# Attention stage: the low part of the queries on GpSimd, gate evictions between maxima and scalings, and four gate tiles moved into two pairs behind the convolution

## The reference, cut to what matters

```
h = rms_norm(x);  u = h @ w_in            # columns: V, B, C, Z (conv), q, k, v, z_a, gate_logits
y_c = b_c * causal_depthwise_conv(c_c * v_c) * silu(z_c);   y_a = y_c @ w_conv_out
scores = q @ k.T * scale   (blocks of 128 queries against 256 keys, 16 query heads, 4 key heads)
m = max(max(scores), sink);  p = exp(scores - m) / (sum + exp(sink - m));   o = p @ v
y_b = (o * silu(z_a)) @ w_attn_out
gates = sigmoid(gate_logits + gate_b);  merged = g_a * y_a + g_b * y_b;   x + merged @ w_out
```

## Time and profile before

| what | value |
|---|---|
| median of 3 runs | 2354.08 us (2352.46 to 2355.7) |
| profiled execution: its time, its span | 2355.41 us, 2353.7 us |
| PE busy | 2329.4 us, 99% of the span |
| DVE busy | 1616.4 us, 69% |
| ACT busy | 1029.6 us, 44% |
| GpSimd busy | 160.4 us, 7% |

### The profile page before, as it was taken

How to read it: one execution, slowest core, us unless ns; L and a number is a source line. 1 busy time by engine, 2 the same in 40 slices (tenths; PEclk the granted TensorE clock), 3 DMA queues, 4 the chain that set the end, 5 groups by cost and what they waited for, 6 DMA issues and landing times.

```text
span 2353.7 us, 30640 instructions
## 1 busy us (share of the span) xinstructions
PE 2329.4 (99%) x11180; PEld 1936.9 (82%) x11180; DVE 1616.4 (69%) x2561; ACT 1029.6 (44%) x1795; POOL 160.4 (7%) x227
## 2 busy tenths in 40 slices
PE   8999999999999999999999999999999999999998
PEld 6778888888888888888788888998888888888786
DVE  6759998567777766736555753473598888886655
ACT  6347666343443434422243343363355444452334
POOL 1000000100000021121000030021100000001000
PEclk9999999999999999999999999999999999999999
DMA  5112232452332264421110042362122222245333
GB/s 199 45 45 73 81 117 73 143 125 81 105 93 81 90 230 128 151 64 50 45 45 28 24 148 75 96 233 72 50 67 90 80 80 80 80 143 179 102 104 125
DMA packets 255894, 230.64 MB, mean 98 GB/s; under 512 B 7726, under 2 KB 226051, under 8 KB 254754
## 3 DMA queue, kind: packets, MB, share of 16 engines
q1 hardware_dynamic: 233920, 148.39, 20.8%
q0 software_dynamic: 19104, 69.12, 9.1%
q10 hardware_dynamic: 2754, 11.58, 1.5%
HBM read 177.68 MB, written 51.38 MB: 97 GB/s over the span
## 4 chain that ended last, share of the span: by engine, by line
PE 92%; DVE 5%; ACT 1%; DMA 1%; issue 1%; SPq 0%; ACTq 0%; DVEq 0%
PE bank L1194 9%; PE bank L1195 9%; PE bank L1196 9%; PE bank L1851 5%; PE bank L1852 5%; PE bank L1853 5%; PE bank L1429 4%; PE bank L1427 4%; PE bank L1428 4%; PE bank L1379 3%; PE bank L1378 3%; PE bank L1377 3%; PE bank L1662 1%; PE bank L1664 1%; PE bank L1663 1%; PE bank L1353 1%
## 5 line engine op out<-in xcount | busy, mean ns | idle before, releaser
L2027 ACT ACTIVATE whi<-wraw 128x1024 fp32r<-128x1024 f32 (+2 forms) x139 | 139.4, 1003 | 305.8 <-PE bank L1196 184.9
L3168 DVE TENSOR_TENSOR wlo<-wraw,whi 128x1024 fp32r<-128x1024 f32 (+1 forms) x154 | 180.0, 1169 | 110.2 <-ACT whi L2027 104.2
L1377 PE MATMUL bank<-xhi,whi 128*128 128x512 f32 x320 | 124.7, 390 | 0.0
L1379 PE MATMUL bank<-xhi,wlo 128*128 128x512 f32 x320 | 124.6, 389 | 0.0
L1378 PE MATMUL bank<-xlo,whi 128*128 128x512 f32 x320 | 124.6, 389 | 0.0
L1194 PE MATMUL bank<-x2hi,whi 128*128 128x512 f32 x240 | 94.5, 394 | 0.0
L1195 PE MATMUL bank<-x2lo,whi 128*128 128x512 f32 x240 | 94.1, 392 | 0.0
L1196 PE MATMUL bank<-x2hi,wlo 128*128 128x512 f32 x240 | 94.0, 392 | 0.0
L3924 DVE TENSOR_TENSOR resid<-bank,resid 128x512 f32 x32 | 22.1, 691 | 99.1 <-PE bank L1196 97.1
L1851 PE MATMUL bank<-x4hi,a_hi 128*128 128x512 f32 x228 | 88.8, 389 | 0.5 <-ACT ffn_u L2941 0.5
L1851 PE MATMUL bank<-t_hi,s_hi 128*128 128x512 f32 x228 | 88.8, 389 | 0.5 <-DVE t_lo L4321 0.5
(11 more groups left out here) (649 smaller groups left out, 6921.9 us busy)
## 6 DMA issues: line engine op xcount, KB each, us to landing
wraw<-in_w_in_dram SPq DMA_DIRECT2D x85, 512.0 KB, 3.9
wraw<-in_ffn_w_up_dram SPq DMA_DIRECT2D x44, 512.0 KB, 3.8
ffn_spill<-ffn_value SPq DMA_DIRECT2D x22, 512.0 KB, 3.4
filler_spill<-filler POOLq DMA_DIRECT2D x20, 512.0 KB, 2.9
wraw<-in_xattn_wkv_dram SPq DMA_DIRECT2D x16, 512.0 KB, 4.0
wraw<-in_ffn_w_down_dram SPq DMA_DIRECT2D x16, 512.0 KB, 4.4
wraw<-in_ffn_w_down_dram SPq DMA_DIRECT2D x16, 384.0 KB, 3.5
xraw<-in_x_dram SPq DMA_DIRECT2D x4, 1024.0 KB, 10.8
```

The lines of the kernel that those rows point to most:

```text
L1377: pe.matmul(ps(fill_bank(m)), whi[slot][:, k, :], xh, start=(k == 0), stop=False)
L1379: last = pe.matmul(ps(fill_bank(m)), wlo[slot][:, k, :], xh, start=False, stop=(k == KT - 1))
L3168: dve.tensor_tensor(wlo[slot][:, 0:n, :], wraw[slot][:, 0:n, :], whi[slot][:, 0:n, :].bitcast(F32), ALU.subtract).then_inc(s_wlo, 1)
```

## The change

- The low part of the queries, `unit_lo(u)`, goes from DVE to GpSimd, with the same waits and counts; there it stands ahead of the stores of unit u-1, and `store_o` and the load of x follow.
- 16 fillers in place of 20: 12 inside the 32 units (6 steps in each) in place of 16, and four behind as before. The four tiles taken out (two of each gate) become two more pairs behind the convolution: 18 pairs in place of 16.
- DVE evicts a half that is due in unit u-1 between `maxima(u-1)`/`turned_lo(u-2)` and `normalise(u-1)`, also when it is an early one; an early split too is made there, one unit later than before. With 12 tiles, 24 halves fall in 24 of the 32 iterations, always behind the maxima and ahead of the scalings. Of the 11 splits in the units, seven stand behind `sum_o` (DVE iterations 3, 8, 11, 16, 19, 24, 27) and four ahead of the scalings (iterations 6, 14, 22, 30; ACT's part of these falls in units 5, 13, 21, 29).

```diff
-FILL_TILES = [Z_A + n for n in range(8)] + [G_B + n for n in range(6)] + [G_A + n for n in range(6)]
-EXTRA_PAIRS = ((G_B + 6, G_B + 7), (G_A + 6, G_A + 7))
+FILL_TILES = [Z_A + n for n in range(8)] + [G_B + n for n in range(4)] + [G_A + n for n in range(4)]
+EXTRA_PAIRS = tuple((g + n, g + n + 1) for n in (4, 6) for g in (G_B, G_A))
 FILLERS = len(FILL_TILES)
-FILL_IN = 16
+FILL_IN = 12
...
-            for u in range(UNITS):
+            def unit_lo(u):
+
+                b, g = u // KV, u % KV
+                q = 64 * (g % 2)
+                pool.wait_ge(s_phi, u + 1)
+                pool.tensor_tensor(qlo[g % 2][q:q + 64, :].rearrange("p (h n) -> p h n", h=4),
+                                   q32[q:q + 64, g // 2, :, b * P:(b + 1) * P],
+                                   qhd[g % 2][q:q + 64, :].bitcast(F32).rearrange("p (h n) -> p h n", h=4),
+                                   ALU.subtract).then_inc(s_plo, 1)
+
+            def fillers_of(u):
+
                 for m in range(1, 2 * FILL_IN, 2):
                     if HALVES_DONE[m][0] == u:
                         store_filler(m // 2)
+
+            for u in range(UNITS):
+                unit_lo(u)
+                fillers_of(u - 1)
                 if u % KV == 2 and u > KV:
                     store_o(u // KV - 1)
                 if u == 5 * KV:
                     load_x_again(0)
+            fillers_of(UNITS - 1)
             load_x_again(1)
...
                 if u >= 2:
                     turned_lo(u - 2)
-                unit_lo(u)
                 if u >= 1:
+                    halves_due(u - 1, True)
+                    splits_due(u - 1, True)
                     halves_due(u - 1, False)
                     normalise(u - 1, (u - 1) % 2)
...
                 splits_due(u, False)
-                halves_due(u, True)
-                splits_due(u, True)
```

More of the change, by code:

```diff
@@ L590, in hybrid_then_mixer_kernel @@
         RING = 16 * FILLERS // 4
-        BACK = (RING + 16, RING + 16, RING, RING, 16 * 3, 16 * KT, 16 * KT, 32 * KT)
+        BACK = (RING + 16, RING + 16, RING + 16, RING + 16, 16 * 3, 16 * KT, 16 * KT, 32 * KT)
         GATES, VO0 = s_vo_stored, 16 * KT
@@ L3335, in _ @@
                 value_lo(c)
[L3337 to L3344, removed]
             def sum_o(u):
@@ L3436, in _ @@
             maxima(UNITS - 1)
+            turned_lo(UNITS - 2)
+            halves_due(UNITS - 1, True)
+            splits_due(UNITS - 1, True)
             halves_due(UNITS - 1, False)
-            turned_lo(UNITS - 2)
             normalise(UNITS - 1, (UNITS - 1) % 2)
```

## The result

The changed kernel takes 2389.2 us (median of 4 runs, 2387.88 to 2391.5) against 2354.08 before: a ratio of 1.015, 95% interval 1.0133 to 1.0168, so slower by 1.5%. The forecast was 2376.3 with a range of 2358 to 2390: the result lies 0.8 us inside its upper end and above the 2368 to 2384 that the forecast gave its own case. Its sum was made for the profiled execution, and there it said +22.2 us; measured were 2387.88 - 2355.41 = +32.5. The sign and the place were right, a third of the size was missing. One execution of the later kernel e5_splits_behind took 3340 us at a granted clock of 0.65, where the others of all kernels had 0.99 to 1.00, and its ratio leaves it out.

A forecast was written before the change was run, and what follows sets the result against it. The DVE and ACT loop was taken to bound the units: -29.5 us for the attention stage, +38.1 for the pairs and +13.6 for holds made +22.2, so 2376.3 us, range 2358 to 2390.

The forecast's parts named there:

- PE's work, -5.4 us, and the pairs, +38.1: Whole kernel: four tiles less and two convolution pairs more cut PE's work by 5.4 us; the pairs alone add 38.1.
- The loop bounds the units: Units: maxima, exponentials, normalise, sum_o and load_rq on DVE and ACT take 6.85 us plus splits; iterations 3 to 31: 209.6.
- Evictions in the hole cost nothing: DVE waits for ACT's exponentials from 2.25 to 4.47 us after the maxima's start; evictions of 0.61 us there are free.
- The holds, 13.6 us: Units: DVE's small SBUF operations wait for GpSimd's whole unit_lo, 13.6 us in all, bounds 0 and 28.5.
- Behind a split: Seven iterations with a split behind sum_o: the split keeps GpSimd off, so load_rq is not held; 0, up to 10 us.
- Odd copies: Seven plain odd iterations: load_rq starts 0.09 us after GpSimd; half counted as held at 1.2 us, 4.2 in all.
- Even copies: Four plain even iterations: load_rq starts inside unit_lo and is held, +0.95 us each, 3.8 in all.
- Behind `store_o`: Seven iterations: unit_lo, late after the store's issue, meets the maxima's small operations; 0.8 us each, 5.6 in all.
- Head -2.0: First units: PE would save 4.1 us; half, 2.0, was estimated, with bounds 0 and 4.1.
- The second: Units: all odd copies held and GpSimd slipping in behind each split; +36, 2390 us; chance 0.12.
- Rival 1: Units: the DVE and ACT loop bounds them but GpSimd holds nobody; +8.6 up to +14, 2363 to 2368 us; chance 0.27.
- Rival 3: Units: PE paces them at 6.83 us and keeps its 5.4 us saving; 2348.7 us; chance 0.14.

The follow-up runs named there:

- e5_splits_behind: Changed kernel with load_rq behind the scalings, store_o one unit later and all 11 splits behind sum_o: 2371.74 us, ratio 1.0067 against the kernel before.
- e2: Changed kernel with unit_lo back on DVE behind turned_lo, all else as changed: 2373.36 us, ratio 1.0079 against the kernel before.
- e6: e5_splits_behind without load_rq, the maxima reading their factor from rq itself: 2367.6 us, ratio 1.0051 against the kernel before.
- e1: Changed kernel with load_rq moved from ahead of the maxima to behind the scalings, ahead of sum_o: 2373.11 us, ratio 1.0086 against the kernel before.
- e3: Kernel before with only unit_lo moved to GpSimd, 16 tiles still in the units: 2358.34 us, ratio 1.0017 against the kernel before.
- e4: Changed kernel with load_rq behind the scalings, store_o one unit later, seven splits moved from behind sum_o to ahead of the next scalings: 2373.94 us, ratio 1.0083.
- e7: e6 with 13 filler tiles in the units, three behind, and the last filler's eviction ahead of the convolution's sums: 2358.82 us, ratio 1.0013 against the kernel before.

## Why the prediction was right or wrong, by its own steps

The direction, the place and the two mechanisms (a loop that PE can't shorten, and GpSimd holding DVE) were right. That 2389.2 us lies in the range is partly luck: the sum was 10 us short, and the range reached it because it took in the lower half of a rival with a chance of 0.12.

**PE's work, -5.4 us, and the pairs, +38.1: right.** The pairs stand 19.04 us apart, and PE is busy for all of 500 to 880 us of the changed kernel.

**The loop bounds the units: right, and nearly right in size.** Iterations 3 to 31 without the holds took 232.4 - 22.2 = 210.2 us, forecast 209.6. Plain iterations without a hold took 6.72 and 6.98 us, forecast 6.72 and 6.97; the four with a split in the hole 7.91 in place of 7.77. e2 supports it: without any hold, and with `unit_lo`'s 0.7 us back on DVE, the units take 218.9 us and not PE's 198.

**Evictions in the hole cost nothing: right.** `normalise` (L3388) waits 0.51 us for ACT behind an eviction (L3192) in iteration 16 of the changed kernel, the first two lines of its timeline.

**GpSimd's instruction, 1.35 us, result in time: right.** Its 32 mean 1374 ns, 1.3 free and up to 1.67 where it waits behind a split; no scores waited for it but the very first, 0.91 us in the head.

**The holds, 13.6 us: this step failed; they were 22.2.** By its terms:

- *Behind a split: 0 forecast, 7.9 measured.* This is the step that was wrong in its mechanism. "DVE's split, with two SBUF inputs, keeps GpSimd off, and load_rq is next" is true but for its end: GpSimd was ready at 298.10, 0.09 us after ACT's part, and its 1.66 us are its own 1.31 and some 0.35 of waiting for the split. But then the instruction that had been waiting went first, and the copy behind the split waited for all of it, in seven of seven, at 1.28 us. The page "SBUF — State Buffer" of the Trainium skill, section "Who interferes with whom", says that each of the two locks the other out for a whole instruction, and the traces agree: the copy's 1.29 us and GpSimd's 1.66, which contains its wait for the split.
- *Odd copies: 4.2 forecast, 6.4 measured.* I counted half of them, since GpSimd's lead was only about 0.09 us. It was 0.10, the same in every iteration, and all six that had a `unit_lo` beside them were held. In a loop that repeats exactly, a small lead is a certain one; "half of them" was an average over something that doesn't vary. By the rule on that page of the Trainium skill alone all of them are held, and here the rule was the better guide.
- *Even copies: 3.8 forecast, 3.2 measured.* *Behind `store_o`: 5.6 forecast, 4.7 measured* (0.67 each).

**Head -2.0: too much, it gained 0.6.** M(3) is at 186.18, and 186.76 before. The same holds fall in iteration 2, which the forecast didn't count: the copy takes 1.28 and the small scaling 1.01 us. They are more than the missing 1.4, and e6, which has no copy to hold, begins iteration 3 at 184.96, 1.2 us earlier; but e2 has no holds there and begins it at 187.28, so the head is not settled. **The end, -0.6: it gave 1.1** (32.3 for the spans = -4.7 up to the last maxima + 38.1 - 1.1). This is what is left over of the sum, and I looked for no cause.

Together: 22.2 forecast + 8.6 of holds + 0.6 of the loop + 1.4 at the head - 0.5 at the end = 32.3, measured 32.5 between the profiled executions. The other 2.6 of the distance between the medians is the spread between executions of one kernel (2387.88 to 2391.5).

**The rivals.** The second (all odd copies held, GpSimd slipping in behind each split, 2390 us) is what happened, in its mechanism and nearly in its time; I gave it 0.12 on the word of one argument about order for which the trace before had no row. Rival 1 (GpSimd holds nobody) is excluded by each held copy and by e1, which took only the copy out of its way and won 16 us. Rival 3 (PE paces) is excluded by the 35.9 us of PEld's wait and by e2.

**What is shown and what only argued.** That the holds cost time is shown twice. e1 takes only the copy out of GpSimd's way and gains 16 us, of 17.5 on the timeline; e2 takes all holds away and gains 16 us net, as it puts `unit_lo` back where it overfills the hole. That they cost little behind a slower PE is shown by e3. That 19 us remain without any hold is shown by e2; about 9 of these (218.9 - 210.2) are `unit_lo` in the hole, which leaves about 10 for the changed kernel's loop and pairs, an estimate beside the forecast's 8.6. DVE's part in the loop is shown by e5, where the units follow the splits; e6 took 5.8 us out of it and the units gave 1.2, so by then PE and ACT bound it too. ACT's part is read from its timeline only, as no run shortens it. That a place in the hole is as good as free was my expectation for e4 and fell: it depends on whether the scalings then reach GpSimd's time. I did not try splits in the hole with `unit_lo` at another time, nor one shorter exponential on ACT, which the loop would need to come down to 6.83 us with splits in it.

## What to carry to other kernels

Before work is taken off the engine that sets the pace, find the loop that runs through several engines in order and add it up, iteration by iteration. Here it took 7.2 us a unit without any holds, so 12 of the 39 us that PE gave up in the units were never to be had. Where the two bounds are close, neither average gives the time: in e7 PE needed 7.17 us for a unit and the loop was reckoned at 7.1, and a unit took 7.40. The likely reason, which e6's waits suggest and no run isolates, is that long iterations and short ones don't make up for each other. An operation moved to GpSimd is not gone from VectorE: in this kernel a copy or a scaling from SBUF that falls into it waits until GpSimd's instruction has ended, however small it is, and the place where the two meet must be looked up before the move. If a bound is close, take away a little at a time: against the kernel before, 13 tiles in the units cost 3 us (e7) and 12 cost 12 (e6).

## What the runs showed of the hardware that I had not expected

- A copy of four elements in a partition is held to the end of GpSimd's instruction, as the cast of 128 in the earlier trace rows was: it takes 0.97 to 1.29 us in place of 0.15, by how early it meets it. A scaling of four takes 0.83 and up to 1.06 in place of 0.17; four scalings of 256 take 2.16 in place of 1.14.
- Not held beside the same GpSimd instruction: the maxima (0.53 to 0.55 us throughout) and the sums that read PSUM (0.67 to 0.69).
- When GpSimd's instruction waits behind a DVE instruction with two SBUF inputs, and DVE's next is a copy, GpSimd goes first (7 of 7 in the units 3 to 31 of the changed kernel, and again in e3).
- A lead of 0.10 us (306.26 to 306.36) is enough for GpSimd to hold the copy for the whole of its 1.31 us.
- GpSimd's issue of a store held a copy in one place and not in another: in e4 the copy behind the scalings took 0.42 us beside `o_spill` (three of three); in the kernel before, behind a split, it took 0.16 us inside the same issue (317.25, with the issue at 316.37 for 1.38). The cause was not looked for.
